# Loading an expert's matrices as 16 KB pieces into six 2 MB ring slots, instead of 8 KB and 4 KB pieces into twelve 1 MB slots

## What is computed

```python
def moe(xm, w_router, b_router, w1, b1, w2, b2):
    ...
    logits = (xs @ w_router + b_router).astype(jnp.float32)
    top_v, top_i = lax.top_k(logits, TOP_K)          # 4 of 32
    gates = jax.nn.softmax(top_v, axis=-1)
    ...
    def block_fn(args):
        tok, e = args
        xb = xs[tok]
        hb = clamped_swiglu(xb @ w1[e] + b1[e])      # w1[e]: 1024 x 2048
        return hb @ w2[e] + b2[e]                    # w2[e]: 1024 x 1024
    ...
    y = jnp.zeros((n_tok, d), outs.dtype).at[buf_tok].add(outs)
```

## Time and profile before

| | before |
|---|---|
| timed runs, us | 1197.98, 1198.63, 1201.33 (median 1198.63) |
| the profiled execution, span from first to last instruction, us | 1199.4 |
| the profiled execution's own time, us | not listed apart; its span lies between the first and the last of the timed runs |
| TensorE busy (matmul) | 1097.4 us, 91% |
| VectorE, ScalarE, GpSimd busy | 209.0, 161.1, 27.6 us |
| moved by DMA | 429.38 MB (of 10^6 bytes), 358 GB/s over the span |
| mean granted TensorE clock | 0.984 |
| chain that ended last | TensorE 49%, DMA 26%, SP's queue 17% |

### The profile page before, as it was taken

The page is one execution under the profiler, slowest core; times in us unless marked ns, Lnnn a source line. Parts: engine busy times, 40 slices in busy tenths (PEclk is TensorE's granted clock), DMA queues, the critical chain, the costliest instruction groups (busy, mean ns, idle before and its releaser), DMA issues.

```text
span 1199.4 us, 13087 instructions
## 1 busy us (share of the span) xinstructions
PE 1097.4 (91%) x4957; PEld 456.2 (38%) x4957; DVE 209.0 (17%) x492; ACT 161.1 (13%) x316; POOL 27.6 (2%) x39
## 2 busy tenths in 40 slices
PE   7399978999999999999999998999999999999978
PEld 4156545443434343333333333343433333333334
DVE  2014335111111111111111112111111111111132
ACT  2033331001101010101010101010101010101010
POOL 1011020000000000000000000000000000000000
PEclk9699988999999999999999999999999999999999
DMA  7594304879999999999999999999999999999970
GB/s 207 155 402 168 141 13 175 331 278 414 417 418 418 418 418 418 418 418 417 418 418 418 417 418 418 416 417 418 418 418 418 418 417 418 417 418 417 418 305 35
DMA packets 86223, 429.38 MB, mean 358 GB/s; under 512 B 10648, under 2 KB 11217, under 8 KB 53405
## 3 DMA queue, kind: packets, MB, share of 16 engines
q1 hardware_dynamic: 81744, 427.45, 87.8%
q0 software_dynamic: 848, 1.32, 0.8%
q10 hardware_dynamic: 3612, 0.37, 0.2%
HBM read 427.27 MB, written 1.84 MB: 358 GB/s over the span
## 4 chain that ended last, share of the span: by engine, by line
PE 49%; DMA 26%; SPq 17%; issue 3%; DVE 3%; ACT 2%; ACTq 0%; POOL 0%; POOLq 0%; DVEq 0%
DMA ring<-in_w 23%; PE hidden L792 16%; PE outputs L831 10%; SPq L296 9%; SPq L299 7%; PE sum L600 6%; PE sum L730 4%; DMA ring<-in_w_in 3%; PE sum L585 2%; PE hidden L783 2%; PE tokens L722 2%; PE hidden L870 1%; ACT arena L530 1%; PE hidden L852 1%; PE tokens L870 1%
## 5 line engine op out<-in xcount | busy, mean ns | idle before, releaser
L792 PE MATMUL hidden<-ring,arena 128*64 128x512 f32 x2008 | 448.6, 595 | 26.1 <-DMA ring<-in_w 26.1
L792 PEld LDWEIGHTS hidden<-ring,arena 128*64 128x64 f32 x2008 | 138.9, 137 | 330.4 <-issue 249.5
L831 PE MATMUL outputs<-ring,arena 128*64 128x512 f32 x1024 | 226.8, 595 | 11.6 <-ACT arena L530 11.6
L1173 DVE TENSOR_SCALAR arena<-hidden 128x512 f32<-128x512 f32 x32 | 22.1, 691 | 741.2 <-PE hidden L792 741.2
L831 PEld LDWEIGHTS outputs<-ring,arena 128*64 128x64 f32 x1024 | 70.7, 137 | 145.3 <-issue 127.9
L600 PE MATMUL sum<-ring,aT 128*128 128x512 f32 x192 | 87.3, 609 | 18.9 <-DMA ring<-in_w_in 18.9
L525 ACT ACTIVATE arena<-arena 128x512 f32<-128x512 f32 x32 | 20.1, 629 | 509.7 <-DVE arena L1173 509.7
L722 PE MATMUL tokens<-arena,xn 128*128 128x128 f32 x544 | 71.0, 285 | 0.2
L722 PEld LDWEIGHTS tokens<-arena,xn 128*128 128x128 f32 x544 | 64.5, 195 | 17.1 <-issue 13.0
L730 PE MATMUL sum<-arena 128*128 128x512 f32 x136 | 62.9, 605 | 1.4 <-ACT arena L534 1.4
L783 PE MATMUL hidden<-arena 128*64 128x512 f32 x256 | 60.5, 593 | 1.6 <-DVE arena L1201 1.6
(11 more groups left out here) (238 smaller groups left out, 492.9 us busy)
## 6 DMA issues: line engine op xcount, KB each, us to landing
ring<-in_w SPq DMA_DIRECT2D x379, 1024.0 KB, 20.7
ring<-in_w_in SPq DMA_DIRECT2D x12, 1024.0 KB, 14.3
wide<-in_w_out SPq DMA_DIRECT2D x1, 4096.0 KB, 24.3
wide<-in_w SPq DMA_DIRECT2D x4, 1024.0 KB, 9.2
wide<-in_w_ple_gate SPq DMA_DIRECT2D x1, 4096.0 KB, 27.6
hres<-in_x SPq DMA_DIRECT2D x2, 512.0 KB, 4.7
aT<-in_w SPq DMA_DIRECT2D x1, 1024.0 KB, 7.3
arena<-in_w_ple_proj SPq DMA_DIRECT2D x1, 1024.0 KB, 5.0
```

The costliest lines, as they stand in the source:

```text
L792: ins = mm(H[u * SLOTS:(u + 1) * SLOTS, g * 512:(g + 1) * 512], xsel[:, k, i * SLOTS:(i + 1) * SLOTS], chunk(k, i)[:, c0:c0 + 512], start= ...
L831: ins = mm(TB[u * SLOTS:(u + 1) * SLOTS, :], hT[:, k % 4, (k // 4) * SLOTS:(k // 4 + 1) * SLOTS], chunk(c, i)[:, c0:c0 + 512], start=(k == ...
```

## The change

`ring` keeps its size but has six slots of 2 MB. A slot of `w1` takes 256 rows, a slot of `w2` 512 rows, and partition `p` takes neighbouring rows: rows 2p and 2p+1 of the slot's block of `w1`, or rows 4p to 4p+3 of that of `w2`, 16 KB in one piece from memory into one place in the partition. So step `k` of a product no longer holds the rows 128k to 128k+127 but every second (or fourth) row of a block, and what is multiplied with them has to follow: the gather and the transposes for the router take every second column of `xn`, the transposes of `prod` every fourth column, the gains and the router's weights are loaded in that order. The number and the shape of the matmuls stay. Item 1's early chunks are two of 2 MB in `wide`; the one in `aT` is gone, so 4 MB come early.

```diff
-RING = 12
-CH = 2048
+RING = 6
+W1C = 4
+CH = 4096
...
-EARLY = 5
+EARLY = 2
...
             def load(e, c, dst):
 
-                if c < KD:
-                    sp.dma_start(dst, w1[e, c * P:(c + 1) * P, :]).then_inc(chunk_loaded[c], 16)
+                if c < W1C:
+                    src = w1[e, c * 2 * P:(c + 1) * 2 * P, :].rearrange("(p r) n -> p (r n)", r=2)
                 else:
-                    j = c - KD
-                    sp.dma_start(dst.rearrange("p (k n) -> p k n", k=2),
-                                 rows(w2[e, 2 * j * P:2 * (j + 1) * P, :])).then_inc(chunk_loaded[c], 16)
+                    j = c - W1C
+                    src = w2[e, j * 4 * P:(j + 1) * 4 * P, :].rearrange("(p r) n -> p (r n)", r=4)
+                sp.dma_start(dst, src).then_inc(chunk_loaded[c], 16)
...
             sp.wait_ge(s["out_done"], 4)
-            for c in range(4):
+            for c in range(EARLY):
                 load(1, c, early[c])
-            sp.wait_ge(s["logitsT_done"], TT)
-            load(1, 4, early[4])
...
+            def cols(k, kk):
+
+                if k == 1:
+                    return slice(kk // 2 * 2 * P + kk % 2, (kk // 2 + 1) * 2 * P, 2)
+                return slice(kk * P, (kk + 1) * P)
...
-                        ins = mm(GB[:, k * P:(k + 1) * P], xn[:, tt, (4 * b + k) * P:(4 * b + k + 1) * P],
+                        ins = mm(GB[:, k * P:(k + 1) * P], xn[:, tt, cols(1, 4 * b + k)],
...
-                        pe.wait_ge(chunk_loaded[k], (2 * p + (i + 1)) * 16)
+                        if k % 2 == 0:
+                            pe.wait_ge(chunk_loaded[k // 2], (2 * p + (i + 1)) * 16)
...
-                                         xsel[:, k, i * SLOTS:(i + 1) * SLOTS], chunk(k, i)[:, c0:c0 + 512],
+                                         xsel[:, k, i * SLOTS:(i + 1) * SLOTS], chunk(k // 2, i)[:, c0:c0 + 512],
...
-                        ins.then_inc(s["chunk_used"], 1)
+                        if k % 2:
+                            ins.then_inc(s["chunk_used"], 1)
...
-                        ins = tr(TB[:, k * P:(k + 1) * P], prod[:, k * P:(k + 1) * P], ident[:, :])
+                        ins = tr(TB[:, k * P:(k + 1) * P], prod[:, k:4 * P:4], ident[:, :])
...
-                        if k % 2:
+                        if k % 4 == 3:
                             ins.then_inc(s["chunk_used"], 1)
```

More of the change, by code:

```diff
@@ L221, in build @@
         x_loaded = [sem(f"x_loaded{i}") for i in range(TT)]
-        win_loaded = [sem(f"win_loaded{i}") for i in range(RING)]
+        win_loaded = [sem(f"win_loaded{i}") for i in range(2 * RING)]
         chunk_loaded = [sem(f"chunk_loaded{i}") for i in range(RING)]
@@ L267, in gate_bank, with half_slot @@
             return bank[:, 0:n]
-        early = [wide[:, 2 * c:2 * c + 2, :].rearrange("p k n -> p (k n)") for c in range(4)]
-        early.append(aT[:, :, :].rearrange("p k t -> p (k t)"))
+        early = [wide[:, 4 * c:4 * c + 4, :].rearrange("p k n -> p (k n)") for c in range(EARLY)]
+        def half_slot(c):
+            return ring[:, c // 2, (c % 2) * (CH // 2):(c % 2 + 1) * (CH // 2)]
         block = ctx.enter_context(nc.Block())
@@ L279, in _ @@
                 sp.dma_start(hres[:, tt, :], x[tt * P:(tt + 1) * P, :]).then_inc(x_loaded[tt], 16)
-            for c in range(RING):
-                g, half = c // 2, c % 2
+            for c in range(2 * RING):
+                g, low = c // 2, c % 2 * 512
                 if c == 0:
@@ L288, in _ @@
                     sp.wait_ge(s["head_loaded"], 16 * 11)
-                src = rows(w_in[half * 512:(half + 1) * 512, GROUP_COL[g]:GROUP_COL[g] + GROUP])
-                sp.dma_start(ring[:, c, :].rearrange("p (k n) -> p k n", k=4), src).then_inc(win_loaded[c], 16)
+                src = rows(w_in[low:low + 512, GROUP_COL[g]:GROUP_COL[g] + GROUP])
+                sp.dma_start(half_slot(c).rearrange("p (k n) -> p k n", k=4), src).then_inc(win_loaded[c], 16)
             sp.dma_start(wide[:, :, :], rows(a["w_out"][0])).then_inc(s["wout_loaded"], 16)
             def load(e, c, dst):
-                if c < KD:
-                    sp.dma_start(dst, w1[e, c * P:(c + 1) * P, :]).then_inc(chunk_loaded[c], 16)
-                else:
-                    j = c - KD
-                    sp.dma_start(dst.rearrange("p (k n) -> p k n", k=2),
-                                 rows(w2[e, 2 * j * P:2 * (j + 1) * P, :])).then_inc(chunk_loaded[c], 16)
+                if c < W1C:
+                    src = w1[e, c * 2 * P:(c + 1) * 2 * P, :].rearrange("(p r) n -> p (r n)", r=2)
+                else:
+                    j = c - W1C
+                    src = w2[e, j * 4 * P:(j + 1) * 4 * P, :].rearrange("(p r) n -> p (r n)", r=4)
+                sp.dma_start(dst, src).then_inc(chunk_loaded[c], 16)
             def load_item(e, before, chunks=range(RING)):
@@ L438, in _ @@
                                                      [[0, P], [1, HD]])).then_inc(s["head_loaded"], 16)
-            act.dma_start(wr[:, :, :], rows(a["w_router"][0])).then_inc(s["router_loaded"], 16)
+            act.dma_start(wr[:, :, :].rearrange("p (c r) n -> p c (r n)", r=2),
+                          a["w_router"][0].rearrange("(c p r) n -> p c (r n)", p=P, r=2)).then_inc(s["router_loaded"], 16)
             act.wait_ge(s["vrow_T"], 1)
@@ L545, in _ @@
             pe.wait_ge(s["vec_loaded"], 16 * 5)
-            tr(B[0][:, 0:3 * KD], grow[0:3 * KD, :], ident[0:3 * KD, 0:3 * KD]).then_inc(s["gcols_T"], 1)
+            tr(B[0][:, 0:3 * KD], grow[0:3 * KD, :], ident[0:3 * KD, 0:3 * KD])
+            for r in range(2):
+                ins = tr(B[0][:, KD + r:2 * KD:2], gpair[0:4, r:2 * P:2], ident[0:4, 0:4])
+            ins.then_inc(s["gcols_T"], 1)
             pe.wait_ge(s["masked_bucket"], 1)
@@ L600, in _ @@
                         ins = mm(B[i % 2][:, :], aT[:, k, tt * P:(tt + 1) * P],
-                                 ring[:, 2 * g + k // 4, (k % 4) * GROUP:(k % 4 + 1) * GROUP],
+                                 half_slot(2 * g + k // 4)[:, (k % 4) * GROUP:(k % 4 + 1) * GROUP],
                                  start=(k == 0), stop=(k == KD - 1))
@@ L1224, in _ @@
             for q, (tt, c0, n) in enumerate(PARTS):
-                g = ring[:, q, 0:n]
+                g = half_slot(q)[:, 0:n]
                 dve.wait_ge(s["sigmoid_ready"], q + 1)
```

22 lines of the change are left out of this document (12 added, 10 removed).

## The result

| | before | after |
|---|---|---|
| timed runs, us | 1196.92 to 1201.33, median 1198.31 (4) | 1180.39 to 1181.08, median **1180.61** (4) |
| ratio, with its 95% interval | | 0.985 [0.9836, 0.9864] |
| span of the profiled execution | 1199.4 | 1178.7 |
| its own time | 1201.33 | 1180.45 |
| TensorE busy (matmul) | 1097.4, 91% | 1093.8, 93% |

The forecast was 1180.2 us. An execution's own time turned out to be 1.75 us (after) or 1.93 us (before) more than its span, so the profiled execution of before was the slowest of its four runs. That is why the spans differ by 20.7 us and the medians by 17.7.

What follows compares the result with a forecast made beforehand. The loads' pace, 30.11 us per item, was taken to bound the kernel. Piece size -21.8, last slot +1.7 and first refill +1.7 sum to -18.4 us, giving 1180.2 us; the forecast's own range 1175 to 1187, overall range 1173 to 1197.

Steps and rivals of the forecast that it cites:

- The bound: Item loop: the loads set the pace at 30.11 us per item, while TensorE needs 28.0 us.
- Piece size: Weight loads in the item loop: 48 pieces per engine and item instead of 128, at 9.9 ns each, -21.8 us.
- The line through two sizes: Piece cost of 9.9 ns from the 4 KB and 8 KB rates, extended to 16 KB pieces: 428 GB/s.
- Last slot: End of the item loop: 3.5 us of matmuls follow the last `w1` slot's landing instead of 1.74, +1.7 us.
- first refill: Start of the stream: slot 0 comes free later and one megabyte less comes early, +1.7 us, between 0 and +4.2.
- Everything else: Fewer issues and waits, reordered gains, strided weight loads in the gather and the transposes of `prod`: taken as zero.
- cover: Extra TensorE time in the item loop that waits for loads can hide: 0.6 us per item.
- Rival 1: The DMA rate doesn't rise with longer pieces: 1195.6 to 1202.0 us, 11 in 100.
- Rival 2: Strided weight loads, mainly in the gather, make TensorE the bound: +35 us, 1234 us at full price, 12 in 100.
- point of no gain: Added TensorE time per item beyond which the kernel is slower than before: +1.2 us.
- Rival 3: The coarser ring starves DMA, 1209 us at 1 us of gap per item, or waits cool TensorE; 3 in 100.
- clock half: TensorE's longer single waits, up to 1.4 us instead of 0.55, cool it; 3 in 100 together with DMA starving.

Runs made afterwards that it cites:

- experiment 1: The changed kernel with its six 2 MB slots, but the pieces and row order of the kernel before; 1202.39 us, 1.0023.
- experiment 4: The changed kernel with contiguous weight loads in the item loop's gather and the transposes of `prod`; 1180.41 us, 0.9845.
- experiment 2: The changed kernel with each slot of `w1` read by two loads in 4 KB pieces; 1208.01 us, 1.0071.
- experiment 3: The kernel before with `w2` in 8 KB pieces of neighbouring rows and `prod` transposes taking every second column; 1190.23 us, 0.9926.
- experiment 8: The changed kernel with the item loop's gather at a stride of four columns instead of two; 1211.16 us, 1.0102.
- 5: The changed kernel with the second half of each gather in the item loop done twice; 1191.72 us, 0.9938.
- 6: The changed kernel with the second half of each gather in the item loop done three times; 1221.54 us, 1.0184.
- 7: The changed kernel with three slots of 4 MB, `w1` in 32 KB pieces and `w2` in two of 16 KB; 1211.46 us, 1.0104.
- experiment 9: The kernel with three 4 MB slots, but VectorE writes `xn` in step order so the gather reads contiguous columns; 1188.06 us, 0.9915.

## Why the prediction was right

**The bound.** Read rightly: the loads' pace set the time before and sets it after. What decided was TensorE's timeline, and not the busy shares, by which 91% and "full" would have allowed either.

**Piece size, -21.8 us.** Shown. From experiment 1 to the changed kernel only pieces and order change: 947.0 to 925.0 is -22.0 us. The strides that came with the order cost nothing (experiment 4). The pace is 29.37 against 29.36, the rate 428 against 428. The line through two sizes held at 48, 96, 144 and 32 pieces per item (the table above). That it is the number of pieces and neither the matrix nor the distance of the rows rests on experiments 2 and 3. The profile's count of packets agrees: experiment 1 has 83142, after 41670, 41472 fewer, and that is the 32 x 80 x 16 = 40960 pieces of the experts that went, and 512 of the router's weights. What the 9.9 ns are made of was not tried.

The Trainium skill (DMA: Bandwidth & Descriptors, Anatomy of one DMA) prices one load, issued from GpSimd, at about 2.0 us plus its bytes over 436 GB/s. Carried over to this queue, which is SyncE's, and added up load by load as the prediction tried it, it fails: experiment 1, with half as many loads, should have moved bytes faster. Its rate stayed at 418 GB/s: with several loads in the queue the fixed part costs nothing here.

**Last slot and first refill, +3.4 us together.** Experiment 1 has +2.8. Their split was not measured; the windows from 245 us on only show that the gaps take in most of the missing megabyte, as the prediction had it.

**Everything else at nothing.** Right for the time, for the reason given (cover). But the profile after was to show no price for the strides, 1.86 us for the gather's loads and 0.42 for the transposes' four, and it shows 1.96 and 0.56: the gather takes 2.15 us instead of 2.05, one load of the transposes 208 ns instead of 141. Two items without waits for loads took 56.11 us (266.82 - 210.71) where they took 56.01: 0.05 us per item, since part of the longer gather falls into TensorE's wait for VectorE. The cover is 0.54 us, and had been put at 0.6.

The Trainium skill (Advanced Engine Details and Errata, SBUF Cachelines) asks for at least two hits in a line of 16 bytes; by that a float32 stride of two would be free and one of four not. For the gather the traces agree: a load takes 199 ns on average at stride two, 328 at four, 195 at one. For the transposes of `prod` it does not: in experiment 3 they have a stride of two and take 207 ns, as much as the 208 at four.

**Rival 1** (the rate doesn't rise) is refuted by the 428 GB/s, and by the count of packets a 16 KB piece is not cut up on its way. **Rival 2** (strided loads make TensorE the bound) did not happen, but experiment 8 shows it real: with the stride of four the kernel is slower than before, 1.0102. Its price was put at 1.9 us per item for the gathers and is 1.4; its 1234 us would have been about 1211. Its point of no gain, 1.2 us per item, lies below that, as the experiment's sign has it. The change stayed clear of it by taking two rows of `w1` to a partition instead of four. **Rival 3** (a dry ring) did not happen at 2 MB; at 4 MB a small form of it did, 3.4 us just after the embedding's block. Its clock half was not seen in the items, where the clock is 1.00. The fall after the last item, +1.7 us, can't be put down to the slots: experiment 4 has the same slots and took 7.11 us there.

**The base and the tail.** The item stage, which is what the forecast was about, was off by 0.8 us. The rest of the closeness is luck. The start of item 0, foreseen unchanged, moved by -3.2 us. The tail was to stay at 41 us and took 43.0: +1.7. And the profiled execution of before was 2.7 us above the median, not 0.8 (its span lacks 1.93 us of its time), so that the step from the span to the median was off by +2.7 in all. -0.8 - 3.2 + 1.7 + 2.7 is +0.4, the whole difference between 1180.2 and 1180.61. The start of item 0 doesn't follow the slots or the pieces but the granted clock from 155 to 215 us: 210.15 at 0.91 (experiment 2), 210.36 at 0.91 (4), 210.71 at 0.91 (after), 211.24 at 0.89 (5), 212.14 at 0.89 (3), 212.78 at 0.86 (6), 213.02 at 0.86 (1), 213.92 at 0.86 (before). In experiments 7, 8 and 9 the work in this stretch differs (215.18, 215.26, 213.60).

## What to carry to other kernels

Where a stream of loads sets the pace, count the pieces that each DMA engine handles, not the loads: two rates in one trace give the price of a piece, and it can be carried to other sizes. Take the longest piece that the layout allows, but price what follows from the order of the rows: here a stride of two in the weight loads was nearly free, while one of four cost more than the whole gain. And look at what the coarser slots cost where the consumer pauses: 4 MB slots had the best rate and lost it again at the start, the end and one pause.

## What the runs showed of the hardware

- A piece costs each DMA engine about 9.9 ns over its bytes for sizes from 4 to 32 KB; the number and size of loads, 1 or 2 MB, did not matter to the rate (417 and 418 GB/s).
- TensorE's weight load of 128 x 128 float32 at a stride of four columns: 328 ns against 199 at a stride of two and 195 at one in the gather, where its sixteen matmuls take 4.00, 2.15 and 2.05 us. In the transposes a stride of two costs as much as one of four: 207 and 208 ns against 141.
- How long an issue takes SyncE's queue differs between these kernels. The slots of `w1` (min/median/max ns), before and after:

```profile
L296 SPq DMA_DIRECT2D ring<-in_w x251: 327/880/5164, 65.8 to 1118.8; - x126
```

```profile
L305 SPq DMA_DIRECT2D ring<-in_w x190: 327/333/5132, 65.0 to 1106.0; - x190
```

  The second row counts the slots of `w2` too. The median fell from 880 to 333 ns. In experiment 3, where only the pieces of `w2` are longer, it is 333 too; in experiment 1, with as many pieces as before, it is 373. So the number of pieces alone doesn't explain it, and the cause is open. It decided nothing here, since the loads were issued well ahead of their turn in both.
- The first sixteen matmuls of the gate after the last item took 7.11, 8.80 or 10.04 us (before, after, experiment 9), in before and after with the same waits ahead of them (1.35, 1.69 and 1.21 us). The clock was at its lower level in part of it, 0.72 in the window of after. Why it falls in one execution and not in another was not settled.
